# Attention over head pairs: order of maximum, exponential, scaling and transposes, of the head norms, and of the mask loads

## The reference, cut

```
h = rms_norm(x, attn_norm_g[l])
z = h @ w_in[l]                              # qa 8 heads, ka, va 2 heads; qb, kb, vb 8 heads; ga, gb gates
qa = apply_rope(rms_norm(qa, q_norm_a)); ka = apply_rope(rms_norm(ka, k_norm_a))
ya = window_gqa(qa, ka, va, sink_a) @ w_proj_a      # band of three tiles of 128 keys, a sink per head
qb = rms_norm(qb, q_norm_b); kb = rms_norm(kb, k_norm_b)
yb = neighbourhood_attn(qb, kb, vb, rel_bias_b) @ w_proj_b   # relative bias and mask
x = x + (sigmoid(ga) * ya + sigmoid(gb) * yb) @ w_out
x = x + (silu(h2 @ w_gate) * (h2 @ w_up)) @ w_down          # h2 = rms_norm(x, ffn_norm_g)
```

## Time and profile before

| | |
|---|---|
| median of 3 runs | 3836.65 us (3836.37 to 3838.88) |
| the profiled execution | 3835.18 us, its span 3833.3 us |
| TensorE busy | 3465.8 us, 90% of the span; mean granted clock 0.957 |
| VectorE, ScalarE, GpSimd busy | 2156.9 (56%), 1266.9 (33%), 551.7 (14%) us |
| DMA | 344.45 MB, mean 90 GB/s |
| the attention loop of the first layer | 89 to about 390 us |
| that of the second layer | 932 to about 1233 us |

### The profile page before, as it was taken

The page is one execution under the profiler, slowest core; times in us unless marked ns, Lnnn a source line. Parts: engine busy times, 40 slices in busy tenths (PEclk is TensorE's granted clock), DMA queues, the critical chain, the costliest instruction groups (busy, mean ns, idle before and its releaser), DMA issues. The chain is left out here.

```text
span 3833.3 us, 38929 instructions
## 1 busy us (share of the span) xinstructions
PE 3465.8 (90%) x15368; PEld 2720.8 (71%) x15368; DVE 2156.9 (56%) x2738; ACT 1266.9 (33%) x1619; POOL 551.7 (14%) x459
## 2 busy tenths in 40 slices
PE   6678999998778999996988998999989889989998
PEld 4455778886556778875776786788667767858885
DVE  7544376546444476534887534654567874355545
ACT  4445332223545332222323222432332223223332
POOL 1011221221111231121100111100020001111000
PEclk9889999999889999998999999999999999999999
DMA  3012345421021444322211222222211112222221
GB/s 112 22 37 58 126 176 198 154 88 66 34 46 54 143 186 189 131 80 81 74 59 44 71 94 89 88 99 89 87 56 68 58 50 72 95 71 93 99 98 56
DMA packets 72181, 344.45 MB, mean 90 GB/s; under 512 B 25152, under 2 KB 26048, under 8 KB 35648
## 3 DMA queue, kind: packets, MB, share of 16 engines
q1 hardware_dynamic: 70272, 339.51, 25.6%
q0 software_dynamic: 432, 1.28, 0.1%
q10 hardware_dynamic: 1296, 1.16, 0.1%
HBM read 340.51 MB, written 2.10 MB: 89 GB/s over the span
## 5 line engine op out<-in xcount | busy, mean ns | idle before, releaser
L756 PE MATMUL bank_b<-Hhi_b,whi_b 128*128 128x512 f32 x2976 | 1242.6, 418 | 126.6 <-POOL Hlo_b L836 43.5
L757 PE MATMUL bank_b<-Hlo_b,whi_b 128*128 128x512 f32 x2976 | 1187.1, 399 | 0.0
L758 PE MATMUL bank_b<-Hhi_b,wlo_b 128*128 128x512 f32 x2976 | 1185.6, 398 | 0.0
L735 DVE TENSOR_TENSOR wlo_b<-raw_b,whi_b 128x2048 fp32r<-128x2048 f32 (+2 forms) x290 | 626.1, 2159 | 574.0 <-ACT whi_b L729 573.8
L756 PEld LDWEIGHTS bank_b<-Hhi_b,whi_b 128*128 128x128 f32 x2976 | 577.1, 194 | 294.7 <-issue 119.1
L757 PEld LDWEIGHTS bank_b<-Hlo_b,whi_b 128*128 128x128 f32 x2976 | 577.7, 194 | 126.0 <-issue 12.7
L758 PEld LDWEIGHTS bank_b<-Hhi_b,wlo_b 128*128 128x128 f32 x2976 | 574.9, 193 | 126.9
L729 ACT ACTIVATE whi_b<-raw_b 128x2048 fp32r<-128x2048 f32 (+2 forms) x290 | 511.4, 1764 | 422.9 <-PE bank_b L758 403.4
L756 PE MATMUL bank_b<-Uhi_b,whi_b 128*128 128x512 f32 x1024 | 411.2, 402 | 0.0
L758 PE MATMUL bank_b<-Uhi_b,wlo_b 128*128 128x512 f32 x1024 | 404.4, 395 | 0.0
L757 PE MATMUL bank_b<-Ulo_b,whi_b 128*128 128x512 f32 x1024 | 404.2, 395 | 0.0
(11 more groups left out here) (207 smaller groups left out, 3465.4 us busy)
## 6 DMA issues: line engine op xcount, KB each, us to landing
raw_b<-in_w SPq DMA_DIRECT2D x234, 1024.0 KB, 4.9
ada_b<-in_wada SPq DMA_DIRECT2D x48, 1024.0 KB, 6.9
raw_b<-in_w SPq DMA_DIRECT2D x40, 512.0 KB, 3.7
raw_b<-in_w SPq DMA_DIRECT2D x16, 768.0 KB, 4.2
rel_b<-in_rel SPq DMA_DIRECT2D x128, 24.0 KB, 2.3
X_keep<-in_x SPq DMA_DIRECT2D x4, 512.0 KB, 9.0
out<-X_keep SPq DMA_DIRECT2D x8, 256.0 KB, 2.0
cond_b<-in_c SPq DMA_DIRECT2D x2, 512.0 KB, 4.3
```

The lines of the kernel that those rows point to most:

```text
L735: self.nc.vector.tensor_tensor(self.wlo[n % RAW_SLOTS][:, 0:words], self.raw[n % RAW_SLOTS][:, 0:words], self.whi[n % HI_SLOTS][:, 0:words ...
L756: self.nc.tensor.matmul(out, whi[:, k, cols], xhi, start=(k == 0), stop=False)
L757: self.nc.tensor.matmul(out, whi[:, k, cols], xlo, start=False, stop=False)
L758: mm = self.nc.tensor.matmul(out, wlo[:, k, cols], xhi, start=False, stop=(k == nk - 1))
```

## The change

The step loop runs two steps further (34 turns instead of 33) and its order within step i is now

```
@@ schedule_one
+    s.load_ahead(0)
+    s.loads.append(("masks", None, 0, None))
     for c in range(DC):
         s.add("h", 0, "attn", c)
         if c == 1:
             s.begin(0)
-    s.split_ahead(1)
-    s.add("tables")
     for c in range(DC):
         rms_sum(s, 0, "attn", c)
-    s.add("sines")
+        if c == 4:
+            s.split_ahead(1)
+    s.add("tables")
...
-        def finish(c):
+        def head_sum(c):
...
             if c < 5:
                 s.small.take(("rot", l, c))
                 s.temp("t1", 2, ("t1", l, c))
+                s.add("rot", l, c)
+
+        def head_scale(c):
+
+            if c < 5:
                 s.temp("t2", 1, ("t2", l, c))
                 s.add("rope", l, c)
-            else:
+            elif 5 < c < 14:
                 s.add("scale", l, c)
+        def finish(*cs):
+            for c in cs:
+                head_sum(c)
+            for c in cs:
+                head_scale(c)
...
             if p == 0:
                 rms_root(s, l, "attn")
+            if l == 0 and p == 0:
+                s.add("sines")
...
             def then(job):
                 evacuate(job[2])
                 lag.append(job[2])
+                if len(lag) > 1:
+                    head_sum(lag[-2])
                 if len(lag) > 2:
-                    finish(lag.pop(0))
+                    head_scale(lag[-3])
...
-        gap(8)
-        for c in Z_FIRST[2]:
-            finish(c)
+        gap(3)
+        finish(*Z_FIRST[2])
+        gap(13)
...
+        load_bias_pair(A_HEADS // 2)
         pace = paced(2 * HALF)
-        for i in range(len(STEPS) + 1):
+        for i in range(len(STEPS) + 2):
             if i == HALF:
                 gap(len(todo))
-                while lag:
-                    finish(lag.pop(0))
-                load_bias_pair(A_HEADS // 2)
-                bias_pair(A_HEADS // 2)
+                head_sum(lag[-1])
             if i < len(STEPS):
...
                 s.add("score", l, i)
-                next(pace)
-                s.add("soft", l, i)
-            if i == HALF + 1:
+            if 1 <= i <= len(STEPS):
+                s.add("soft2", l, i - 1)
+            next(pace)
+            if i == HALF + 2:
                 n = mix_pieces(s, todo, n, l, 0, 2)
-                pace = paced(2 * HALF - 2)
-            if i >= 1:
-                before = STEPS[i - 1]
+                pace = paced(2 * HALF - 3)
+            if i >= 2:
+                before = STEPS[i - 2]
...
-                s.add("tp", l, i - 1)
-                next(pace)
+                s.add("tp", l, i - 2)
             if i < len(STEPS):
-                s.add("soft2", l, i)
-            if i >= 1:
-                s.add("pv", l, i - 1)
+                s.add("soft", l, i)
+            next(pace)
+            if i >= 2:
+                s.add("pv", l, i - 2)
                 if before[1] == TT - 1:
                     s.add("evy", l, before[0])
+            if i == HALF - 2:
+                bias_pair(A_HEADS // 2)
@@ block_one
+        k.rs = [qa, mem.put("rs", [P, SEQ])]
-        k.rs = shared("rs", bm_at, 2)
+        def invert(dve, l, c):
+
+            r = k.rs[slot("rs", ("rs", l, c))][:]
+            dve.wait_ge(*after("root", l, c))
+            nc.vector.reciprocal(r, r).then_inc(*mark("dve", ("recip", l, c)))
+            dve.wait_ge(*after("recip", l, c))
+            def load_masks():
+
+                sp.dma_start(maskA[:], d["maskA"]).then_inc(mask_landed, 16)
+                sp.dma_start(maskB[:], d["maskB"]).then_inc(mask_landed, 16)
...
                 elif kind == "ss":
-                    dve.wait_ge(*after("root", l, c))
-                    nc.vector.reciprocal(rs, rs).then_inc(*mark("dve", ("recip", "rs", l, c)))
...
                 elif kind == "scale":
-                    dve.wait_ge(*after("recip", "rs", l, c))
+                    invert(dve, l, c)
...
                 elif kind == "rope":
+                    invert(dve, l, c)
...
                     if i == 0:
 
                         dve.wait_ge(*after("qk", l, 3))
+                        dve.wait_ge(mask_landed, 32)
```

More of the change, by code:

```diff
@@ L56 @@
 V2, NV2 = offsets(VEC2)
-NCONST1, NREST = 2, 9
+NCONST1, NREST = 2, 7
 X_PARTS = 4
@@ L270, in schedule_one @@
             if p > 0:
-                for c in Z_FIRST[p - 1]:
-                    finish(c)
+                finish(*Z_FIRST[p - 1])
         todo, ada, ada_done = [], [], []
@@ L705, in reuse, with load_panels @@
             eng.wait_ge(*self.steps.after("free", prev))
-    def load_panels(self, sp, weights, load_bias=None, load_cond=None, load_ada=None, load_x=None):
+    def load_panels(self, sp, weights, load_bias=None, load_cond=None, load_ada=None, load_x=None, load_masks=None):
         for kind, src, words, n in self.s.loads:
@@ L710, in load_panels @@
                 load_x(src)
+            if kind == "masks":
+                load_masks()
             if kind == "bias":
@@ L919, in block_one @@
         const_landed, rest_landed, gain_landed = sem("const_landed"), sem("rest_landed"), sem("gain_landed")
+        mask_landed = sem("mask_landed")
         x_landed = [sem(f"x_landed{i}") for i in range(X_PARTS)]
@@ L1026, in load_ada @@
                 sp.dma_start(ada[j % 2][:], d["wada"][l * ADA_PANELS + j]).then_inc(ada_landed[j % 2], 16)
-            k.load_panels(sp, d["w1"], load_bias, load_cond, load_ada, load_x)
+            k.load_panels(sp, d["w1"], load_bias, load_cond, load_ada, load_x, load_masks)
         @block.gpsimd
@@ L1047, in _ @@
                     nc.gpsimd.tensor_tensor(g, g, RX[:], ALU.mult).then_inc(*mark("pool", ("silu", l, c)))
-                elif kind == "rope":
+                elif kind == "rot":
                     l, c = a
@@ L1076, in _ @@
             rest = ((keep.ident[:], d["ident"]), (bd64[:], d["bd64"]), (rot64[:], d["rot64"]),
-                    (bada[:], d["bada"]), (maskA[:], d["maskA"]), (maskB[:], d["maskB"]), (invt[:], d["inv64"]),
+                    (bada[:], d["bada"]), (invt[:], d["inv64"]),
                     (keep.eps[EPS2][:], d["eps2"]), (pos_i[:], d["pos1"].partition_broadcast(P)))
@@ L1084, in _ @@
                 if kind == "sines":
-                    act.wait_ge(rest_landed, 16 * NREST)
                     build_tables(nc, None, act, steps, "tab1", None, None, [t[:] for t in tab_tmp], cos[:], sin[:], None)
@@ L1428, in _ @@
                     k.products(pe, seen, *a)
-                elif kind == "tables":
+                elif kind == "sines":
                     pe.wait_ge(rest_landed, 16 * NREST)
```

## The result

The changed kernel took 3659.7 us as a median, against 3836.5 us for the kernel before on the same chip: a ratio of 0.9538, with a 95% interval of 0.952 to 0.9557. That is 176.8 us gained where 153 were forecast. One of its four runs took 3914.9 us, at a mean granted clock of 0.84 against 0.97 in the others; it is in the median and not in the ratio. The profiled execution took 3656.9 us (span 3655.1), 178.3 less than that of before.

What follows compares the result with a forecast made beforehand. TensorE sets the pace, but in attention it waits and runs at a lower clock. 2 x (57 + 22 - 3) + 1 = 153 us off 3835.2 gives 3682 us; own range 3655 to 3712, 8 in 10 3640 to 3750.

Steps and rivals of the forecast that it cites:

- Before score 0: Before the step loop: VectorE gains 13.3 us of work, loses 4 of waits; first maximum at 949.8, TensorE at 938.5.
- The cycle of the first half: First-half step loop: two steps with one norm take 12.1 us, TensorE's own work 11.0; gain 57 us a layer.
- the 2 us that I took off for the clock: First half: 2 us taken off the gain for the clock after the stall at the start.
- Second half: Second half of attention: transposes two steps after scores, copies ahead of exponentials; 122 instead of 144 us, gain 22.
- I leave 7 idle and 4 clock: Second half: 11 us left above TensorE's 111 at full clock, for remaining waits and lower clock.
- the line on the panels: Second half: weight panels behind bias loads need 15.5 us against 12; 3 to 4 us reaches ScalarE twice.
- Contention: First half: GpSimd's scalings meet VectorE's splits and norms; three meetings, 3 us a layer lost.
- Start: Kernel start: TensorE's wait for the position load moves behind the first product; resumption at 42.9, 1.2 us gained once.
- A: Rival: in-order engines lock harder, first-half cycle 15.4 us, second half gains 15; 3736 us, chance 0.23.
- B: Rival: everything is hidden in both halves, gain 205 us; 3630 us, chance 0.12.
- C: Rival: slower, each first-half step waits for a round of all engines, 16 us instead of 10.4; about 4015, chance 0.03.
- D: Rival: no change, VectorE's arrears from two early norms eat what the loop gains; 3835 us, chance 0.04.

Runs made afterwards that it cites:

- e10_after_again: The changed kernel run once more, unaltered; 3656.1 us, ratio to the kernel before 0.9514 to 0.954.
- e8: The changed kernel with the mixing's pieces begun one step earlier in the second half (step 17 instead of 18); 3673.8 us.
- e4: The changed kernel with the old start (tables and split ahead of squares, masks in ScalarE's load queue, old wait for loads); 3657.1 us.
- e6: The changed kernel with the reciprocal of chunks 6 to 13 done twice on VectorE in each layer; 3725.0 us.
- e5: The changed kernel without VectorE's reciprocal in the norms of chunks 6 to 13 of each layer; 3627.2 us.

## Why the prediction held, step by step

The time, 3659.7 us, lies in the forecast's own range (3655 to 3712), 22 us under its middle value. Of the signs that I had named, all of the right ones came: no reciprocal waits for a root, transposes wait 1.7 us a half for scalings (under 8 foreseen) and value products 1.8 and 2.4 for copies (under 10), the clock is 0.98 and 1.00 (over 0.95), and score 16 of layer two stands at 1038.8 in the time of the kernel before (1040).

**Before score 0.** Right. In the time of the kernel before (91.1 us added, layer one's gain) TensorE reached score 0 of layer two at 940.1, with 938.5 forecast, and VectorE its first maximum at 859.37 + 91.1 = 950.5, with 949.8 forecast (its terms, 940.3 + 13.3 - 4, make 949.6). TensorE then stood 2.6 us for a mean square and 1.8 for maxima, as the arrears said:

```profile
855.06 3.34 DVE L1012 RECIPROCAL rs_b<-rs_b 128x512 f32<-128x512 f32 x1
858.44 1.09 DVE L1294 TENSOR_TENSOR QB_b<-qn_b,rs_b 128x512 f32<-128x512 f32 x1
859.37 0.45 DVE L1365 CUSTOM_DVE_ANT_0 sc_b<-bank_b,maskA_b,vec_b 128x256 f32<-128x256 f32 x1
```

**The cycle of the first half.** Right in sum, 12.0 against 12.1, but by luck: two errors cancel. The intervals between odd scores go 11.2, 13.1, 11.2, 13.1, 11.3: the long ones hold a weight split, which I had called hidden in VectorE's wait for the sum of squares. Part of VectorE's timeline in a long one, in the changed kernel:

```profile
128.19 2.27 DVE L753 TENSOR_TENSOR wlo_b<-raw_b,whi_b 128x2048 fp32r<-128x2048 f32 x1
...
134.09 0.69 DVE L1285 SCALAR_TENSOR_TENSOR qa_b<-bank_b,EQ_b 128x512 f32<-128x512 f32 x1 [2.02 <-PE bank_b L1474]
134.70 3.34 DVE L1012 RECIPROCAL rs_b<-rs_b 128x512 f32<-128x512 f32 x1
138.07 1.15 DVE L1294 TENSOR_TENSOR KB_b<-qn_b,rs_b 128x512 f32<-128x512 f32 x1
139.06 0.68 DVE L1395 TENSOR_TENSOR Ulo_b<-bank_b,Uhi_b 128x512 fp32r<-128x512 f32 x1
139.66 0.60 DVE L1365 CUSTOM_DVE_ANT_0 sc_b<-bank_b,maskA_b,vec_b 128x384 f32<-128x384 f32 x1
```

The split does not stand in the wait. It stands ahead of the maxima, which begin as soon as it ends (130.38), and VectorE waits 2.02 us for the sum all the same. The finished values' split (L1395), which I did not count, stands ahead of the next maxima too. On the other side the cycle without them is 11.2, shorter than my 12.1: from the maxima of an odd step (141.89) to the end of those of the even one (about 152.1) it is 10.2 us, not 11.0, with 0.9 for the maxima instead of 1.3, and the next score follows at once (152.19). Score 16 came at 1038.8 in the time of before, with 1040 forecast, and in this execution the 2 us that I took off for the clock were too much: 60.7 us a layer against 57. In e10_after_again, the same program, layer two's half took 3.2 us more at a lower clock, so there they would have been right. My full-clock count of TensorE's work also stands: 32 pieces x 1.48, 34 for the steps and 6 for the sums make 87, and without reciprocals the half took 85.0.

**Second half.** The mechanism was right, a size was off: 28.6 us against 22. The term that was off is the remainder, "I leave 7 idle and 4 clock". It measured 3.1 us of waits at a clock of 1.00; with these in place of its 11 the sum would give 29.9, so 1.3 us stay unexplained. Behind it is the line on the panels, "about 15.5 us of issue and landing against 12". The 12 came from steps of 5.5 to 6 us, those of a first half without norms; the steps of the second half carry more pieces and last 6.2 to 7.8 (scores at 204.43, 211.21, 219.04, 225.30, 231.52 and 239.32). From the first load of the second batch to the use of the panel behind it were 17.5 us (210.24 to 227.76), and the panels were about 3 us early and not 3 to 4 late. That the term exists at all, and is worth about what I had set as the lower bound (10 us a layer), e8 showed.

**Contention.** Forecast 3 us a layer, in the form of three weight splits stretched as in the earlier trace rows. Three meetings with splits came, and one with the masks, but the other engine lost: five splits from 95 to 194 us took 2278 ns on average, and the pairs of scalings that began just behind a split took 2.89 us instead of 0.93 (the split of 128.19 us is shown above). GpSimd's timeline, with one of three such pairs (the others begin at 152.67 and 177.07) and an undisturbed one, and TensorE's wait behind the first:

```profile
128.36 2.89 POOL L1094 TENSOR_SCALAR sc_b<-sc_b,rec_b 128x256 f32<-128x256 f32 x2 [7.17 <-DVE rec_b L1387]
132.16 0.93 POOL L1094 TENSOR_SCALAR sc_b<-sc_b,rec_b 128x256 f32<-128x256 f32 x2 [0.91 <-DVE rec_b L1387]
```

```profile
130.95 0.86 PE L1522 MATMUL bank_b<-ident_keep,sc_b 128*128 128x128 f32 x4 [0.55 <-POOL sc_b L1094]
```

The four meetings cost GpSimd 7 us a layer (30 scalings at 776 instead of 531 ns), and TensorE waited 1.7 us in all for them. By the Trainium skill ("SBUF — State Buffer", section "SBUF: two separate sides") such meetings hold one engine for a whole instruction of the other; the longer scalings agree with it. The 14 us a layer that I worked out as its result had all 32 scalings met such an operation did not show: four pairs of fifteen did, and the scalings now have a step of room.

**Start.** First product at 13.18 (before 19.73), resumption at 42.91, with 42.9 forecast; to meet it that closely is luck, since the unaltered kernel resumed at 43.67 in e10_after_again. The gain, 1.8 against 1.2, is below what timed runs can tell, as e4 shows.

**The sum.** 2 x (60.7 + 28.6) + 1.8 = 180.4 us against 153. Of the 27.4 between them 13.2 are the second half's size, 7.4 the first half's, 0.8 the start's (1 stood in the sum), and 6 the contention's term: what the meetings cost, 1.7 us a layer, is already within the 60.7. Behind the last landmark the profiled execution loses 2.1 us again, in parts that the change doesn't touch; in e10_after_again it is 0.2, so this is no effect of the change.

**The rivals.** A (the engines lock harder, 15.4 us a cycle) did not come: the changed kernel's cycle is 12.0, and only e6, with 3.35 us more on VectorE in each, has one that long (16.1). B (all hidden) is nearest in the second half; in the first, the 13.7 us of VectorE that e5 takes away speak against it. C and D did not come. What I set beside A and B of the clock was misread in one point: the waits of the second half before were fewer, not shorter (8 of up to 6.1 us, beside 5.7 in the example). That the short gaps of the cycle leave the upper level throughout held in the changed kernel's profile (waits of 0.5 to 0.6 us, a granted clock of 1.00 from 116.7 to 176.6 us) and not in e10_after_again, where the same cycles of layer two had 0.94 (872 to 932 us).

## What to carry to other kernels

Where every engine works through its list in order, a chain through four of them is hidden by giving each link one more step of distance and by putting the short operations that others wait for ahead of the long ones: the order of the steps alone gave 127 of 177 us, with no instruction removed, and some 19 of these by the later start of the mixing (an estimate from e8's 9.5 us a layer). Judge a late transfer by the length of the slots it falls in, not by their number, and ask also what its place in the queue waits for: here one step of distance decided over 10 us a layer, with 3 us to spare, and about half of that was the queue. And before more work is moved off an engine, measure its floor by leaving that work out: 26.8 us less on VectorE gave 13.7.

## What the runs showed of the hardware

The granted clock differs from run to run where nothing else does. The same program with the same waits to 0.1 us ran layer two's first half at 0.98 in one execution and 0.95 in another, and took 3.2 us longer there. The waits of 0.5 to 2.6 us at its beginning were there in both, so a difference of 3 us between two kernels in such a stretch does not by itself tell anything of their instructions.

The price of a longer wait was above its own length: with 26.8 us more on VectorE, the half took 31.1 and 34.9 us more, at a granted clock of 0.88 instead of 0.98.

Where a scaling of GpSimd began behind a weight split of VectorE, the split kept its 2.28 us and the pair of scalings took 2.89 us instead of 0.93; in the earlier trace rows it was the split that was longer, 3.36 instead of 2.29. In the earlier trace rows GpSimd's product had begun at 65.59 us and the split at 66.16; here the split had begun at 128.19 and the scaling at 128.36. Each time the operation that began second was the longer one.

A load of 512 KB landed 3.7 and 4.0 us after its issue in the changed kernel, 4.6 in e8_mix_earlier, and 16 small loads ahead of it held SyncE's queue for 10.2 to 11.0 us.

Between executions the first product's start moved with the landing of the first loads: from 13.02 to 14.48 us among the kernels with the new start, and from 19.73 to 21.52 among those with the old one; so differences of that size before score 0 say nothing of a kernel.
